# Three mixer layers on one core: the roundings of outputs and output weights in the last attention head, placed at other steps and on another engine

## The reference

```python
def attend(qblk):
    s = jnp.einsum('bqhd,bkhd->bhqk', qblk, k, preferred_element_type=jnp.float32) * scale
    p = jax.nn.softmax(s, axis=-1)
    return jnp.einsum('bhqk,bkhd->bqhd', p.astype(v.dtype), v)
...
y_attn = latent_attention(...) * jax.nn.silu(g_attn)
y = jnp.einsum('bsm,md->bsd', jnp.concatenate([y_pool, y_attn], axis=-1), w_out[l])
h = h + gate[:, None, :] * y
```

## Time and profile before

| what | value |
|---|---|
| time, median of 3 runs (lowest, highest) | 2511.5 us (2510.46, 2511.74) |
| profiled execution: its time, its span | 2513.0 us, 2511.1 us |
| PE busy | 2455.8 us, 98% |
| DVE, ACT, POOL busy | 1620.3 us, 1111.1 us, 1221.9 us |
| granted PE clock in the 40 slices | 9 of 10 tenths or more in each |
| the last head, turn 56 to turn 63 | 2392.5 to 2422.5 us of the span |
| last values, then the rest of the output product | from 2428.9 us; from 2430.8 us |

### The profile page before, as it was taken

One profiled execution on the slowest core, in us unless ns is written; L12 is line 12 of the kernel. 1 busy time (PEld: TensorE's weight loads), 2 busy tenths in 40 slices (PEclk: granted clock), 3 DMA queues, 4 the chain that ended last, 5 costly groups with the idle time before them and its releaser, 6 DMA issues.

```text
span 2511.1 us, 38631 instructions
## 1 busy us (share of the span) xinstructions
PE 2455.8 (98%) x15068; PEld 2154.1 (86%) x15068; DVE 1620.3 (65%) x2189; ACT 1111.1 (44%) x2060; POOL 1221.9 (49%) x873
## 2 busy tenths in 40 slices
PE   6999999999999999999999999999999999899999
PEld 5888898865588899999998899999988888688887
DVE  6966656487533399795876335666434679888864
ACT  4322223334444342222223336777534434788861
POOL 1545545430044455554455445565454455566664
PEclk9999999999999999999999999999999999999999
DMA  6454544484034334442333357454134353200034
GB/s 261 147 177 140 191 143 165 153 312 138 27 109 157 110 132 151 165 147 93 110 109 118 109 156 208 133 156 117 61 122 159 105 171 98 91 1 1 1 119 158
DMA packets 239472, 327.89 MB, mean 131 GB/s; under 512 B 19246, under 2 KB 172078, under 8 KB 237500
## 3 DMA queue, kind: packets, MB, share of 16 engines
q1 hardware_dynamic: 237820, 325.32, 39.1%
q10 hardware_dynamic: 1472, 0.10, 0.0%
HBM read 246.06 MB, written 79.33 MB: 130 GB/s over the span
## 4 chain that ended last, share of the span: by engine, by line
PE 87%; DVE 8%; issue 2%; ACT 1%; DMA 1%; SPq 0%; POOL 0%; DVEq 0%; ACTq 0%
PE ps L1042 22%; PE ps L1044 22%; PE ps L1043 22%; PE ps L1345 4%; PE ps L1485 2%; PE ps L1333 2%; PE ps L1467 2%; PE ps L1261 2%; PE ps L1280 2%; DVE s_raw L2056 1%; PE ps L1274 1%; PE ps L1185 1%; DVE s_lo L2043 1%; PE ps L1056 1%; DVE raw L2073 1%
## 5 line engine op out<-in xcount | busy, mean ns | idle before, releaser
L932 POOL TENSOR_TENSOR w_lo<-raw,w_hi 128x512 fp32r<-128x512 f32 (+1 forms) x570 | 825.6, 1456 | 1006.7 <-ACT w_hi L1567 1006.0
L1567 ACT ACTIVATE w_hi<-raw 128x512 fp32r<-128x512 f32 (+1 forms) x574 | 355.4, 628 | 1008.5 <-PE ps L1044 796.7
L1042 PE MATMUL ps<-w_hi,s_hi 128*128 128x256 f32 (+1 forms) x1088 | 308.6, 284 | 1.6 <-DVE s_lo L2043 1.3
L1043 PE MATMUL ps<-w_lo,s_hi 128*128 128x256 f32 (+1 forms) x1088 | 307.3, 282 | 0.0
L1044 PE MATMUL ps<-w_hi,s_lo 128*128 128x256 f32 (+1 forms) x1088 | 307.3, 282 | 0.0
L2087 DVE TENSOR_TENSOR u<-u,ps 128x1024 f32<-128x1024 f32 (+1 forms) x128 | 155.3, 1213 | 184.6 <-PE ps L1044 180.2
L1042 PE MATMUL ps<-w_hi,a_hi 128*128 128x256 f32 (+1 forms) x816 | 230.6, 283 | 0.0
L1043 PE MATMUL ps<-w_lo,a_hi 128*128 128x256 f32 (+1 forms) x816 | 230.5, 283 | 0.0
L1044 PE MATMUL ps<-w_hi,a_lo 128*128 128x256 f32 (+1 forms) x816 | 230.5, 282 | 0.0
L2073 DVE TENSOR_TENSOR raw<-raw 128x1024 f32<-128x1024 f32 (+1 forms) x128 | 179.6, 1403 | 60.1 <-DMA raw<-in_w 57.2
L1042 PEld LDWEIGHTS ps<-w_hi,s_hi 128*128 128x128 f32 x1088 | 208.7, 192 | 9.9 <-issue 9.4
(11 more groups left out here) (320 smaller groups left out, 5966.3 us busy)
## 6 DMA issues: line engine op xcount, KB each, us to landing
raw<-in_w SPq DMA_DIRECT2D x191, 512.0 KB, 4.5
ada_c<-in_ada SPq DMA_DIRECT2D x14, 2304.0 KB, 10.4
blk<-u SPq DMA_DIRECT2D x62, 512.0 KB, 3.2
blk<-c SPq DMA_DIRECT2D x31, 512.0 KB, 3.9
blk<-m1s SPq DMA_DIRECT2D x31, 512.0 KB, 3.3
ada_first<-in_ada SPq DMA_DIRECT2D x12, 768.0 KB, 16.3
r_g<-blk SPq DMA_DIRECT2D x8, 1024.0 KB, 9.7
r_v<-blk SPq DMA_DIRECT2D x4, 2048.0 KB, 12.8
```

What stands on the lines that cost most here:

```text
L932: pool.tensor_tensor(w_ring(w_lo, n), w_source(n), w_ring(w_hi, n).bitcast(F32), ALU.subtract)\
L1042: pe.matmul(out, a_hi_, b_hi_, start=first, stop=False, skip_group_check=True)
L1043: pe.matmul(out, a_hi_, b_lo_, start=False, stop=False, skip_group_check=True)
L1567: act.activation(w_ring(w_hi, n), w_source(n), ACT.Copy).then_inc(w_rounded, 1)
```

## The change

ACT's small tasks in the last head are placed anew, two of its weight roundings go to DVE, and pairs 2 and 3 are rounded and split later.

| task | before | after |
|---|---|---|
| round pair 0, pair 1 (ACT) | steps 55, 56 | steps 55, 57 |
| round weights 0 to 3 | ACT, steps 57 (ahead of the turned copies), 57, 58, 59 | 0 and 1: ACT, steps 58, 59; 2 and 3: DVE, steps 57, 59 |
| split weights 0 to 3 (POOL) | steps 58, 59, 60, 61, each behind its own rounding | 0: step 59; 1 and 2: step 60; 3: step 61; each behind all four roundings |
| round pairs 2, 3 (ACT) | end of step 62 | end of step 63 |
| split pairs 2, 3 (DVE) | end of step 62 | behind `l_add(7, 1)` |

`w_rounded` is one count. Since two engines now add to it, a count of n+1 no longer says that slot n is the one that is rounded, and `low` waits for the count that means all four.

```diff
@@ gpsimd
             def low(n):
-                pool.wait_ge(w_rounded, n + 1)
+                pool.wait_ge(w_rounded, OUT[2, 0] + RING if n in range(OUT[2, 0], OUT[2, 0] + RING) else n + 1)
...
-                        if 58 <= e < 62:
-                            low(n + e - 58)
+                        for m in {59: (0,), 60: (1, 2), 61: (3,)}.get(e, ()):
+                            low(n + m)
@@ scalar
                     if h and i == 1:
                         l_other_half(h - 1, 1)
-                        if h == LH - 1:
-                            hi(OUT[2, 0])
...
-                    if 57 <= e < 60:
-                        hi(OUT[2, 0] + e - 56)
-                    if e in (55, 56):
-                        o_round_pair(2, 0, e - 55)
-                    if e == LH * NT - 2:
+                    if e in (58, 59):
+                        hi(OUT[2, 0] + e - 58)
+                    if e in (55, 57):
+                        o_round_pair(2, 0, (e - 55) // 2)
+                    if e == LH * NT - 1:
                         for kp in (2, 3):
                             o_round_pair(2, 0, kp)
@@ vector
                     if e in (56, 58):
                         o_split_pair(2, 0, (e - 56) // 2)
-                    if e == LH * NT - 2:
-                        for kp in (2, 3):
-                            o_split_pair(2, 0, kp)
+                    if e in (57, 59):
+                        n = OUT[2, 0] + 2 + (e - 57) // 2
+                        j, count = raw_pair(2, 1)
+                        dve.wait_ge(ld[j], 16 * count)
+                        dve.wait_ge(w_used, n - RING + 1)
+                        dve.tensor_copy(w_ring(w_hi, n), w_source(n)).then_inc(w_rounded, 1)
                 l_add(LH - 1, 1)
+                for kp in (2, 3):
+                    o_split_pair(2, 0, kp)
                 outputs(2)
```

## The result

The changed kernel takes 2521.8 us (median of 5 runs, 2520.93 to 2522.23), the kernel before 2511.5 us (median of 5, 2510.46 to 2511.74). The ratio is 1.0041, with a 95% interval of 1.003 to 1.0052: 10.3 us slower. 2521.6 us was forecast.

The account below looks back on a forecast made before the run. PE, busy nearly throughout, was taken to bound the kernel, so other engines count only where PE waits. The terms 4.1 + 1.5 + 2.85 + 1.6 = 10.05 us took 2511.5 to 2521.6 us; range 2518.0 to 2526.5 us.

Parts of the forecast that it names:

- Turn 58 only 0.43 us earlier: Last head: DVE's split of pair 0 stays in front, so PE's turn 58 starts at 2400.76, 0.43 us earlier.
- Turn 60: POOL's first weight split waits for all four roundings and holds norm 60, so PE's turn 60 starts 4.1 us later.
- The forecast's own bound for copies of 0.34 us: DVE's two weight roundings: taking 0.34 us each instead of 0.48 would move the forecast by -0.2 us.
- POOL first: Norm 59 gets SBUF ahead of DVE's first copy, which waits 1.9 us; turn 60 comes 2 later: 2523.6 us, 10%.
- The clock: PE's clock falls to half behind the gaps at turn 60 and k = 4, costing 1.5 and 1.6 us.
- The tail: Pair 2's split, now behind the last add, makes PE's first matmul of k = 4 wait: +2.85 us.
- The gap at turn 58 with its clock: PE's wait for DVE at turn 58 and the half clock behind it: worth 2.0 + 1.5 = 3.5 us.
- Rival (c): The stall at turn 58 goes and nothing comes for it: 2508.0 us, 3%.
- the four terms of the sum: Wait at turn 60 4.1, clock behind it 1.5, late pair 2 2.85, clock behind that 1.6: 10.05 us.

Follow-up runs that it names:

- e2: Changed kernel, but DVE's two roundings add to a count of their own and each POOL weight split waits for its own rounding alone: 2518.4 us.
- e6: Changed kernel with pairs 2 and 3 split ahead of the last add and all weights rounded by step 58, POOL still waiting for all four: 2515.2 us.
- e8: Changed kernel with pairs 2 and 3 split ahead of the last add and all four POOL weight splits in step 61, behind norm 61: 2514.1 us.
- e4: Kernel before with POOL's weight splits in steps 59, 60, 60, 61, each behind all four roundings, no copy on DVE: 2517.8 us.
- e5: Kernel before with pairs 2 and 3 rounded in step 63 and split behind the last add: 2515.5 us.
- e10: Kernel before, unchanged, run once more for a second profile; no separate median given, last matmul differs by 0.19 us between its two profiles.
- e7: Kernel before with ACT's roundings and DVE's pair splits spread over steps 55 to 59, each weight split behind its own rounding: 2512.4 us.
- e9: As e7, but with pair 0 rounded by ACT in step 54 and split by DVE in step 55: 2512.4 us.
- e3: Changed kernel with both an own count for DVE's roundings and pairs 2 and 3 split ahead of the last add: 2514.3 us.
- e1: Changed kernel with DVE splitting pairs 2 and 3 in step 63 ahead of the last add, all else as changed: 2519.5 us.

## Why the prediction was right

**Turn 58 only 0.43 us earlier.** Measured 0.46. DVE's split of pair 0 stayed in its place, and freeing ACT gave no more than DVE's wait for it had been.

**Turn 60.** Forecast +4.1, measured +3.83. The order of events was as walked: maxima, exponentials, reciprocal, copy, split, norm. The copy took 0.42 us instead of 0.48, and DVE's next instruction began 0.34 us behind its start. With both copies in the chain that is 0.14 + 0.06 = 0.20 of the missing 0.27 us. (The forecast's own bound for copies of 0.34 us, -0.2, should by its count have been 2 x 0.14 = -0.28; nothing hangs on it.) e2, e6 and e8 take the hold away in three ways, by what is counted, by when the last rounding ends and by what stands behind the wait, and turn 60 moved with each; e4 makes it without the rest of the change.

**POOL first** (rival a) did not happen: the copy of weight 2 started at 2400.26, norm 59 at 2400.49, and the norm took 1.95 us. The forecast allowed it 0.4 us of delay; it needed at most half of it.

**The clock.** 1.5 behind turn 60, measured 1.84 and 1.32 in two profiles; 1.6 behind k = 4, measured 1.7 in three profiles, and 0 in e2. The sizes were right, but the reason given for the second one was not: the clock was to fall because 2.8 us is more than 1.99, and in e2 the same gap left it up. That the term came out in the kernel after is partly luck.

**The tail.** +2.85 forecast, 2.98 or 2.99 measured in each of the four profiles with that order (after, its repeat, e2, e5). Its place was read from the order on DVE, its size from the earlier trace rows.

**What was wrong in it, without moving the sum.** The gap at turn 58 with its clock was said to be worth 3.5 us. That is the gap in PE's records, not what removing it gives: where the clock stayed up (e10) the next queue took the time back at turn 60, and e7, which spreads the same tasks, won 0.44 us. ACT, DVE and POOL are nearly as full as PE in these steps (3.11, 2.71 and 3.12 us busy of 3.20 behind turn 58). Rival (c), 2508.0, was therefore no place the kernel could reach by this. The 0.45 us by which the end of the span moved more than the last matmul is in the last section; the forecast had nothing there.

**The number.** Each of the four terms of the sum was there, and right to within 0.4 us. That the medians meet the forecast to 0.2 us is luck: by the ruler the end of the span moved 10.80 us and not 10.05, and what lies ahead of turn 57 scatters by more than that difference.

## What to carry to other kernels

If two engines share one count, a wait that meant one item means all of them, and its price is what is queued behind the waiting instruction: find the last of the items in time, then the next instruction on the waiting engine and who waits for that. Work moved behind an instruction that waits for PE lands on PE's path if PE's next operand is in it, however idle its engine was before. A gap on the critical engine is an upper end of what can be won, since the queues beside it may be nearly as full.

## What the runs showed that was not expected

**The clock behind gaps of about 2 us.** A gap of 1.99 us was followed by 3.2 us at half clock in the first profile of the kernel before, and gaps of 1.99 (e4), 1.97 (e10) and 2.03 us (e9) by none. It fell behind 1.98 us in e5 and behind 2.01 us in e2 and in e3. Behind the gaps of 1.54 to 1.57 us ahead of turn 58 it stayed up in all eight profiles that have one. So the length of a gap near 2 us did not settle it. Nor did 2.83 us: the same gap ahead of k = 4 took the clock down in the kernel after, its repeat and e5, but not in e2:

```profile
2435.00:2439.00 4.00, 4.00 (x18) 3.32 (x19) 1.99 (x1) 0.63 (x1) 3.92 (x3) 1.00 0.99 379
```

What tells these cases apart stays open.

**The end of the span.** From the start of the last matmul to the end of the span it is 4.34 to 4.40 us in the six profiles of kernels without copies on DVE (before twice, e4, e5, e7, e9) and 4.76 to 5.56 us in the seven with them (after twice, e1, e2, e3, e6, e8), though DVE's last rows are spaced alike in both. The difference lies in the last transfer to `out`. From issue to landing it took 2.0 us in each of the six, and 2.4 or 2.5 us (after, e1, e3, e6) or 3.2 us (the repeat of after, e2, e8) in the seven. In the stretches that hold this transfer the trace has these queues (kind, packets, MB, share of the time of 16 transfer engines), for the kernel after (2517.0 to 2520.4 us):

```profile
q1 hardware_dynamic: 273, 0.49, 39.0%
q14 instruction: 1, 0.01, 0.6%
```

and for the kernel before (2508.0 to 2511.1 us):

```profile
q1 hardware_dynamic: 288, 0.52, 44.8%
```

The one packet of queue q14 brings instructions. One such packet falls into the last 2.7 us of the span in each of the seven profiles with copies and in none of the six without. So the added DVE instructions go with a loading of instructions beside the last transfer, and with 0.4 to 1.2 us more until that transfer has landed. That the packet is what delays it is not shown, since no run moves it alone.

**DVE and POOL at SBUF.** Norms of POOL took 1.89 us alone and 2.79 beside DVE's split of a pair; when the tail brought two pair splits beside POOL's gate, DVE's two took 3.45 us instead of 2.36 and the gate 2.17 instead of 1.29. The Trainium skill (SBUF — State Buffer, "Who interferes with whom") calls the pair of ports that VectorE and GpSimd share an exclusive lock, and says that a VectorE instruction with two SBUF inputs contends with a GpSimd instruction that reads SBUF. The trace agrees: the first split took 1.23 us, as if alone; the gate, begun 0.20 us behind it, ended at 2438.92; the second split ended 1.08 us behind the gate. In the kernel after none of it was on PE's path; in e2, e8 and e10 a POOL instruction stretched beside a split was.
